# Bank-wise row chains, a second tile's input by quads, a mixer's output by tiles, and a conv norm ahead of low parts

## The reference

```python
# first block, for l in range(2)
y = merged @ w_o                       # end of mixer(x, ...)
x = layer_norm(DN_ALPHA * x + y, ln1_g[l], ln1_b[l])
aff = jax.nn.sigmoid((x @ router_w).astype(jnp.float32))      # router, then one-hot and experts
# second block, for l in range(2)
h = rms_norm(x, norm_pre[l, 0])
x = x + 0.5 * rms_norm(swiglu_ffn(h, ...), norm_post[l, 0])   # ffn1
h = rms_norm(x, norm_pre[l, 1])
m = hybrid_mixer(h, ...)               # sum over branches of sigmoid(gate) * (branch @ w_branch)
x = x + rms_norm(m, norm_post[l, 1])
h = rms_norm(x, norm_pre[l, 2])
x = x + 0.5 * rms_norm(swiglu_ffn(h, ...), norm_post[l, 2])   # ffn2
# conv branch of hybrid_mixer
y = depthwise_conv(u, conv_w) + conv_b
yn = (y - mean(y)) * lax.rsqrt(var(y) + NORM_EPS) * ln_g + ln_b
conv_out = jax.nn.silu(yn)
```

## Time and profile before

| | |
|---|---|
| time, median of 3 runs | 2383.12 us (2379.73 to 2384.64) |
| the profiled execution's own time | 2383.86 us |
| its span on the core | 2382.3 us |
| TensorE busy | 2298.4 us, 96% |
| DVE busy | 1755.2 us, 74% |
| ACT busy | 1409.6 us, 59% |
| POOL busy | 236.9 us, 10% |
| mean granted TensorE clock | 0.994 |

### The profile page before, as it was taken

One profiled execution on the slowest core, in us unless ns is written; L12 is line 12 of the kernel. 1 busy time (PEld: TensorE's weight loads), 2 busy tenths in 40 slices (PEclk: granted clock), 3 DMA queues, 4 the chain that ended last, 5 costly groups with the idle time before them and its releaser, 6 DMA issues.

```text
span 2382.3 us, 39448 instructions
## 1 busy us (share of the span) xinstructions
PE 2298.4 (96%) x11114; PEld 1875.9 (79%) x11114; DVE 1755.2 (74%) x2348; ACT 1409.6 (59%) x1892; POOL 236.9 (10%) x296
## 2 busy tenths in 40 slices
PE   9998999999998999999999999999999999989998
PEld 7777788878777788877887867888878877778887
DVE  6778888887778888897556788765565568887555
ACT  5653777774653777774446576454464466765445
POOL 0000000000000000000000692000000008800000
PEclk9999999999999999999999999999999999999999
DMA  7444899985444799995555544565656554455652
GB/s 263 129 144 133 303 340 332 345 326 160 151 135 152 277 336 335 342 333 191 185 185 177 163 140 150 186 205 185 193 188 186 184 179 141 156 170 161 211 184 97
DMA packets 277777, 497.33 MB, mean 209 GB/s; under 512 B 20512, under 2 KB 112848, under 8 KB 277632
## 3 DMA queue, kind: packets, MB, share of 16 engines
q1 hardware_dynamic: 273440, 481.60, 60.6%
q0 software_dynamic: 4192, 14.02, 2.0%
HBM read 494.50 MB, written 1.05 MB: 208 GB/s over the span
## 4 chain that ended last, share of the span: by engine, by line
PE 69%; DVE 14%; DVEq 6%; issue 4%; ACT 3%; DMA 1%; ACTq 1%; PEldq 0%; SPq 0%; PEld 0%; POOLq 0%
PE g_bank L625 14%; PE g_bank L626 13%; PE g_bank L627 13%; PE s_bank L627 8%; PE s_bank L625 8%; PE s_bank L626 8%; DVE w_lo L598 4%; DVE conv_y L2700 2%; DVEq L2694 1%; PE t_bank L1783 1%; DVEq L2304 1%; ACT w_hi L593 1%; PE t_bank L1943 1%; DVE row_max L2328 1%; PE t_bank L1807 0%
## 5 line engine op out<-in xcount | busy, mean ns | idle before, releaser
L598 DVE TENSOR_TENSOR w_lo<-w_raw,w_hi 128x1024 fp32r<-128x1024 f32 x909 | 1095.7, 1235 | 337.0 <-ACT w_hi L593 312.2
L593 ACT ACTIVATE w_hi<-w_raw 128x1024 fp32r<-128x1024 f32 x909 | 944.5, 1058 | 408.1 <-PE g_bank L627 170.3
L625 PE MATMUL g_bank<-w_hi,xt_hi 128*128 128x512 f32 (+1 forms) x1136 | 453.8, 399 | 11.5 <-ACT gate L1401 5.1
L626 PE MATMUL g_bank<-w_lo,xt_hi 128*128 128x512 f32 (+1 forms) x1136 | 442.6, 390 | 0.0
L627 PE MATMUL g_bank<-w_hi,xt_lo 128*128 128x512 f32 (+1 forms) x1136 | 442.4, 389 | 0.0
L625 PEld LDWEIGHTS g_bank<-w_hi,xt_hi 128*128 128x128 f32 x1136 | 215.6, 190 | 67.0 <-issue 13.4
L627 PEld LDWEIGHTS g_bank<-w_hi,xt_lo 128*128 128x128 f32 x1136 | 215.2, 189 | 45.3
L626 PEld LDWEIGHTS g_bank<-w_lo,xt_hi 128*128 128x128 f32 x1136 | 215.6, 190 | 40.3
L625 PE MATMUL s_bank<-w_hi,xt_hi 128*128 128x512 f32 x608 | 240.2, 395 | 0.0
L627 PE MATMUL s_bank<-w_hi,xt_lo 128*128 128x512 f32 x608 | 237.3, 390 | 0.0
L626 PE MATMUL s_bank<-w_lo,xt_hi 128*128 128x512 f32 x608 | 236.9, 390 | 0.0
(11 more groups left out here) (366 smaller groups left out, 2887.2 us busy)
## 6 DMA issues: line engine op xcount, KB each, us to landing
w_raw<-in_w_in_dram SPq DMA_DIRECT2D x192, 512.0 KB, 4.6
w_raw<-in_moe_w_gate_dram SPq DMA_DIRECT2D x128, 512.0 KB, 5.3
w_raw<-in_moe_w_up_dram SPq DMA_DIRECT2D x128, 512.0 KB, 5.6
w_raw<-in_moe_w_down_dram SPq DMA_DIRECT2D x128, 512.0 KB, 5.3
w_raw<-in_ffn_w_gate_dram SPq DMA_DIRECT2D x176, 256.0 KB, 2.9
w_raw<-in_ffn_w_up_dram SPq DMA_DIRECT2D x176, 256.0 KB, 3.1
w_raw<-in_ffn_w_down_dram SPq DMA_DIRECT2D x88, 512.0 KB, 3.4
w_raw<-in_w_branch_dram SPq DMA_DIRECT2D x40, 512.0 KB, 4.4
```

The lines of the kernel that those rows point to most:

```text
L593: nc.scalar.activation(half_of(w_hi, u, h), half_of(w_raw, u, h), ACT.Copy).then_inc(hi_ready, 1)
L598: nc.vector.tensor_tensor(half_of(w_lo, u, h), half_of(w_raw, u, h), half_of(w_hi, u, h).bitcast(F32), ALU.subtract).then_inc(lo_ready, 1)
L625: nc.tensor.matmul(dst, a_hi, b_hi, start=first, stop=False)
L626: nc.tensor.matmul(dst, a_hi, b_lo, start=False, stop=False)
```

## The change

It has four parts.

1. `PLAN2`: at `conv_back` in the second mixer, the two low parts of the unit ahead of it move behind it. On ACT the table set of the silu is loaded behind the conv's root, which takes one ACT_TABLE_LOAD per layer out.
2. End of the first mixer: TensorE completes both banks of tile 0 before the last parts of tile 1, transposes tile 0 between two of tile 1's parts, and makes 5 idle products in place of 11 (12 fewer in both layers together; no other product goes or comes). High and low parts of the weights around it are made in another order.
3. `row_returned`: the scaling of the second bank moves from ahead of the root to between the two halves, and a drain is added behind the first one. ACT's square sums are taken bank by bank, each when its bank is complete, and `down_end` makes TensorE complete one bank after the other in the last part of a feed-forward.
4. In tile 1's chain the low part of the first quad is made between the second update of `x_res` and the second `norm_in` (`between`); it stood behind both.

```diff
@@ plan_mixer2
     out("gate", 3)
-    plain()
+    unit()
+    hi()
     step("conv_back", n_t=2)
+    lo()
     plain()
     step("conv_root")
...
@@ ACT, conv_root
                         act_root(At(8 + 5, (l, 11)))
+                        act.preload_act_table_set("silu_and_others")
...
@@ ACT, end of a feed-forward
-                    act.wait_ge(out_ready, 3 * l + (i + 1))
-                    squares(0, fills, ffn_junk[:, :], 0.5)
+                    for nb in range(2):
+                        act.wait_ge(out_ready, out_at(l, i) + nb + 1)
+                        square(0, nb, fills, ffn_junk[:, :], 0.5)
...
                     split_hi(end, 3)
+                    act.wait_ge(out_ready, out_at(l, i) + 3)
+                    square(1, 0, fills, ffn_junk[:, :], 0.5)
                     unit_is_used(act, d10)
-                    squares(1, fills, ffn_junk[:, :], 0.5)
+                    square(1, 1, fills, ffn_junk[:, :], 0.5)
...
@@ TensorE, end of the first mixer
-                out_unit(0, 1, (0, 1))
+                out_unit(0, 1, (0,))
                 pe.wait_ge(xt_ready, 10 * l + 8)
                 out_unit(1, 0, (0,)).then_inc(wo_ready, 1)
                 out_unit(1, 1, (0,)).then_inc(wo_ready, 1)
+                out_unit(0, 1, (1,))
                 out_unit(1, 0, (1,))
+                x_quads(t + (T_AFTER_MIX1 + 4), 8 * l + 4, 0)
                 out_unit(1, 1, (1,))
...
                     if tt:
                         idle_products(g_wait(spare), 20)
-                    x_quads(t + (T_AFTER_MIX1 + 4), 8 * l + 4, tt)
-                    if tt:
-                        idle_products(g_wait(spare), 11)
+                        x_quads(t + (T_AFTER_MIX1 + 4), 8 * l + 4, tt)
+                        idle_products(g_wait(spare), 5)
...
@@ TensorE, last part of a feed-forward
+                    def down_end(tt):
...
+                        part = slice(tt * P, (tt + 1) * P)
+                        for nb in range(2):
+                            for k in range(2):
+                                half_is_split(d10, k)
+                                c0 = k * DM + nb * 512
+                                last = mm3(g_bank[(f + (4 + 2 * tt + nb)).slot(4)][:, :], ffn_t_hi[:, 1, k, part], ffn_t_lo[:, 1, k, part],
+                                           w_end_hi[:, c0:c0 + 512], w_end_lo[:, c0:c0 + 512], False, k == 1)
+                            if tt and nb:
+                                last.then_inc(w_used, 2)
+                            else:
+                                last.then_inc(out_ready, 1)
...
@@ DVE, row_returned
                     scaled(0)
+                    dve.drain()
                     dve.wait_ge(square_ready, 15 * l + (sq + 2 * tt + 2))
...
                     dve.reciprocal(rstd[:, tt:tt + 1], rstd[:, tt:tt + 1]).then_inc(var_ready, 1)
-                    scaled(1)
-                    dve.drain()
                     dve.wait_ge(rstd_ready, At(8 + n + tt, (l, 11)).value(1, 1))
                     for nb in range(2):
+                        if nb:
+                            scaled(1)
+                            dve.drain()
...
+                        if nb and between is not None:
+                            between()
...
@@ DVE, end of a feed-forward
-                    row_returned(1, n + 1, sq + 1, ffn_y, fills, 0.5, 1, nxt)
+                    row_returned(1, n + 1, sq + 1, ffn_y, fills, 0.5, 1, nxt,
+                                 None if nxt is None else lambda: next_xt(1, nxt, (0,)))
                     if nxt is not None:
-                        next_xt(1, nxt)
+                        next_xt(1, nxt, (1,))
```

More of the change, by code:

```diff
@@ L1188, in _ @@
                 act_xt(t + (T_AFTER_MIX1 + 2), 2, MERGED[1])
-                ahead(u + 27)
-                split_hi(u + 28, AHEAD)
+                split_hi(u + 29, 1)
                 for tt in range(TT):
                     tile_root(tt, At(tt, (l, 4)))
+                    if tt == 0:
+                        split_hi(u + 30, 0)
                     act_xt(t + (T_AFTER_MIX1 + 4 + 2 * tt), 2, TILE[tt])
                 act.preload_act_table_set("sigmoid_and_others")
-                for h in range(2, 4):
+                for h in range(1, 3):
                     split_hi(u + 30, h)
@@ L1199, in _ @@
                 act.drain().then_inc(router_t_ready, 1)
-                split_hi(u + 30, 4)
+                for h in range(3, 5):
+                    split_hi(u + 30, h)
                 R = rounds_loop(act, 1, l + 1)
@@ L1232, in in_root, with square @@
                     act.drain()
-                def squares(tt, fills, junk, factor):
-                    for nb in range(2):
-                        act.activation(junk[:, nb * 512:(nb + 1) * 512], g_bank[fills[tt][nb].slot(4)][:, :], ACT.Square,
-                                       scale=DM ** -0.5 / factor, accum_out=mean_sq[:, tt, nb:nb + 1])
-                        act.drain().then_inc(square_ready, 1)
+                def square(tt, nb, fills, junk, factor):
+                    act.activation(junk[:, nb * 512:(nb + 1) * 512], g_bank[fills[tt][nb].slot(4)][:, :], ACT.Square,
+                                   scale=DM ** -0.5 / factor, accum_out=mean_sq[:, tt, nb:nb + 1])
+                    act.drain().then_inc(square_ready, 1)
                 def root(tt, n):
@@ L1503, in _ @@
                 split_hi(end, 3)
-                unit_is_used(act, u + 38)
-                squares(1, fills, mix_junk, 1.0)
+                for nb in range(2):
+                    unit_is_used(act, u + (37 + nb))
+                    square(1, nb, fills, mix_junk, 1.0)
                 root(1, 6)
@@ L2447, in _ @@
                 make_onehot()
-                split_lo(u + 30, 4)
+                for h in range(3, 5):
+                    split_lo(u + 30, h)
                 def combination():
@@ L2564, in in_root, with row_returned @@
                     fence(dve)
-                def row_returned(tt, n, sq, dst, fills, factor, times, nxt):
+                def row_returned(tt, n, sq, dst, fills, factor, times, nxt, between=None):
                     def scaled(nb):
@@ L2593, in row_returned, with next_xt @@
                         dve.drain().then_inc(x_ready, 1)
-                def next_xt(tt, nxt):
+                def next_xt(tt, nxt, quads=(0, 1)):
                     dst_next, layer, i_next, t_next, n_xt = nxt
-                    dve_xt(t_next + 2 * tt, At(16 * DEPTH + n_xt + 2 * tt, (layer, XT_LAYER2)), 2, [(tt, 0), (tt, 1)], each=True)
+                    at_ = 2 * tt + quads[0]
+                    dve_xt(t_next + at_, At(16 * DEPTH + n_xt + at_, (layer, XT_LAYER2)), 2, [(tt, kq) for kq in quads], each=True)
                 def feed_forward(at, n, sq, i, w, nxt):
```

41 lines of the change are left out of this document (21 added, 20 removed).

## The result

| | before | after |
|---|---|---|
| time, median of 20 runs | 2381.56 us (2379.73 to 2384.64) | 2384.68 us (2382.61 to 2389.37) |
| the profiled execution's own time | 2383.86 us | 2384.01 us |
| its span | 2382.3 us | 2382.4 us |

The ratio of after to before is 1.0016, with an interval of 1.001 to 1.0022: the change makes the kernel slower by a little under 0.2%, 3.1 us by the medians. The forecast of 2384.8 met the time. Part of that is luck: with 20 runs the median of before is 1.6 us lower than the three runs said, and the change costs 3.1 us where the sum had 1.6; the two errors nearly cancel. After also spreads more: its runs cover 6.8 us, those of before 4.9.

The account below looks back on a forecast made before the run. TensorE, busy 2298.4 us or 96% of the span, was taken to bound the kernel. Terms -6.5 - 3.1 + 7.0 + 0.5 + 0.3 + 3.4 = +1.6 gave 2384.8 us against the median 2383.12; range with rivals 2375 to 2391.

Parts of the forecast that it names:

- Conv norm ahead of low parts: Second mixer, twice: TensorE's branch transposes start earlier and a half-clock stretch goes; -6.5 us, bounds -4 to -7.3.
- Rival 3: Slower: at the second mixer's conv, L2778 and the gate bank come later, eating the gain; +8.1 in all, 2391, chance 0.06.
- First mixer by tiles: First mixer's output, twice: tile 1's last update starts 1.5 us earlier and everything behind it moves along; -3.1 us.
- Row chains and quads: Five boundaries between mixers, feed-forwards and layers: tile 1's second quad reaches TensorE 1.4 us later each; +7.0 us.
- The clock: New 2.4 us gaps between quads: two of five boundaries lose 1.7 us each to the 1.2 GHz clock; +3.4, 0 to 8.5.
- Rival 1: Slower: half clock behind all seven longer gaps, five between quads and two at the gate bank; +10, 2393, chance 0.22.
- the chains: Row-chain terms: boundaries +7.0, the last chain ending the program +0.5, tile 0's chain delaying the hidden tile +0.3, clock +3.4.
- Rival 2: Faster: at the boundaries TensorE's second quad comes no later than today; -8.8, 2374.3, chance 0.20.

Follow-up runs that it names:

- experiment 4: Changed kernel with the quad's low part behind both halves again and the second bank's scaling ahead of the root again: 2370.66 us, before 2382.32.
- experiment 1: Kernel before with one part of the change each: row chains 2394.39 us, conv 2376.75, first mixer 2378.78, before 2382.13.
- experiment 2: Changed kernel with the first quad's low part behind the second normed half again at all five boundaries: 2375.91 us, before 2382.13.
- experiment 8: Changed kernel, low part and scaling taken back, plus 14 idle transposes for the gate bank's wait: one unit too early 2371.71 us, at the wait 2370.25.

## Why the prediction was right, point by point

**Conv norm ahead of low parts: right in mechanism, perhaps too large.** The term was -6.5. The stretches are 3.4 and 3.1 us shorter, the waits under 0.8, the silu waits for the vector engine and has no load ahead of it, all as written. Rival 3 (L2778 later) is out: its successor starts at 1480.11, which is 1482.51 less the 2.4 by which after is ahead. But the gate-bank wait of 1.88 was given no price for the clock, "0, with 3.4 as its bound", since it is shorter than the gaps of the earlier trace rows. It lost the clock in both layers of the profiled execution. This is the weakest step. Alone the part measures -5.4, with an interval of -7.9 to -3.6 that still holds -6.5. In that kernel's profile the waits of 1.88 and 1.87 did not lose the clock (1.00 behind both), so the price is a chance and not a threshold, and the 1.1 that are missing can't be put down to it.

**First mixer by tiles: right.** Term -3.1, measured -3.4 alone. The last update was to start at 216.4 and starts at 216.22. The router's products of the first tile, which waited 1.69 for DVE, don't wait for it any more.

**Row chains and quads: right.** The term was +1.4 per boundary. In the trace the second quad comes 1.59 us later behind the first, and the first 0.2 earlier: 1.4. The gap of 2.29 was forecast as 2.3 to 2.4. The drain costs 0.20, not 0.15. Handing the quad over took 0.63 where I had 0.75, so the low part stands right behind the update and not behind a wait for ACT, as I wrote that it would; its own 0.69 and its place in the row did the harm. That what makes the first quad earlier is of no use is shown by experiment 4, where it is 0.2 later again and the kernel faster.

**The clock: near in size, on incomplete evidence.** The term was two of five boundaries at 1.7, +3.4; filling the gaps gave back 4.5. Rival 1, that all seven gaps lose it, didn't come: the profile has one quad gap and two gate-bank gaps, the chains alone three quad gaps. But the prediction counted "two of the three gaps over 2.2" as followed by the lower level. The kernel before has two more, in the second mixer's first part, 2.48 in layer 0 and 2.47 in layer 1 (at 2018.59). Timeline and window of before, layer 0:

```profile
1379.00 0.66 PE L2040 MATMUL t_bank<-const,proj 128*128 128x128 f32 x4 [2.48 <-ACTq L1416]
...
1380.70:1384.10 3.40, 3.40 (x14) 2.69 (x15) 3.40 (x4) 2.97 (x4) 3.23 (x3) 0.50 0.41 113
```

Both were followed by it, so it was four of five, and Rival 1 deserved more than its 0.22 on that evidence.

**The sum.** Conv 1.1 too good, the chains (7.0, 0.5, 0.3 and 3.4, 11.2 in all) 1.1 too small against 12.3, the mixer 0.3 too small a gain: by parts +3.5 where +1.6 was forecast, and +3.1 measured. Each of these misses is smaller than the interval of its run.

The profiled pair differs by only 0.15 because of a gain that is no part of the sum. After is 5.3 us ahead at the start of the second block (the same products of the first feed-forward start at 1092.01 and at 1097.30). Some 3.3 are the first mixers'. Of the other 2.0, 1.5 are the wait at the end of the experts' rounds, 1.82 before and 0.36 after, which experiment 1 found to change by itself. The profiled pair alone would have said that the change costs nothing.

**Rival 2** (the second quad not late, 2374) is out by its own sign: the gap is 2.29 at all five. Its chance of 0.20 was more than its evidence, "L672 slips in beside the update", deserved: in after the low part starts at 1287.65, when the update that began at 1286.90 is over.

## What to carry to other kernels

When a consumer needs two halves before it goes on, judge a reordering by when the second half is ready: here each piece of work put between the halves (a low part, 0.88, and a scaling, 0.78) came out at the consumer nearly one for one, and the earlier first half was worth nothing. Price a wait of TensorE at its length and a chance of the clock behind it, and look whether a later wait takes the loss up. A part that gains can hide one that loses: two parts of this change win 8.4 us together, the third costs 12.3, and only running them alone shows it.

## What the runs showed of the hardware

A wait of the same length loses the clock in one execution and not in the next: of quad gaps of 2.3 us one in five (after), three in five (chains alone) and none in five (after without the drain), of gate-bank waits of 1.88 two of two (after), one of two (after without the drain) and none of two (conv part alone). A gap of 1.48 lost it once (experiment 2). Behind such a loss TensorE ran for 3.4 us at the 1.2 GHz level (windows of 0.50 to 0.62). With idle transposes in the gap (0.33 us of idle time left) the clock was full behind all five, and the time fell by 4.5 us. The Trainium skill (TensorE: Matmul & The Clock Gate, section on HAM oscillation) reports a kernel that fell back at every one of its repeated waits, which were longer than the gaps here; here it was some of them.

What a loss costs depends on what comes next. Behind the gate bank it costs all of its 1.7 us: in layer 1, from that wait's end to the second quad of the next boundary (2191.94 in after, 2188.30 without the drain), it takes 66.97 us in after, with a loss behind the wait, and 65.26 without the drain, with none (1.00). In layer 0, where both lost it, it takes 66.88 and 66.94. In the second mixer's first part it costs nothing, since the next wait for ACT takes it up (2.20 falls to 0.66, experiment 8). The length of the wait just ahead does not decide alone: the clock also fell behind waits of 0.9 (experiment 8). And filling one wait brought nothing in time, 2370.25 against 2370.66, where the clock behind it had been full without the filling as well.
